# The row factors' turnings and the scaling with them two units later in a hybrid attention block

## What is computed

```python
p_cmp = masked_softmax(einsum(q, kc) * scale, cmp_mask)          # NSA: compressed keys
o_cmp = einsum(p_cmp, vc)
p = masked_softmax(einsum(q, k_sel) * scale, sel_mask)           # selected blocks ("slc")
o_slc = einsum(p, v_sel)
p = masked_softmax(einsum(q, kwin) * scale, win_mask)            # window of 512 ("win")
o_win = einsum(p, vwin)
y_a = g0 * o_cmp + g1 * o_slc + g2 * o_win                       # g: sigmoid gates per head
y_b = einsum(masked_softmax(einsum(q_b, k_top) * scale), v_top)  # DSA: indexer's top keys ("dsa")
merged = gate_a * (y_a @ w_branch_nsa) + gate_b * (y_b @ w_branch_dsa)
h = h + merged @ w_out
h = h + (silu(hn @ w_gate) * (hn @ w_up)) @ w_down
```

## Time and profile before

| | us |
|---|---|
| median of three runs | 1616.84 |
| lowest, highest | 1614.45, 1617.58 |
| profiled execution | 1614.37 |
| its span, first to last instruction | 1612.6 |

### The profile page before, as it was taken

One profiled execution on the slowest core, in us unless ns is written; L12 is line 12 of the kernel. 1 busy time (PEld: TensorE's weight loads), 2 busy tenths in 40 slices (PEclk: granted clock), 3 DMA queues, 4 the chain that ended last, 5 costly groups with the idle time before them and its releaser, 6 DMA issues.

```text
span 1612.6 us, 24584 instructions
## 1 busy us (share of the span) xinstructions
PE 1568.7 (97%) x9008; PEld 1326.2 (82%) x9008; DVE 1154.0 (72%) x2021; ACT 649.4 (40%) x1269; POOL 637.4 (40%) x442
## 2 busy tenths in 40 slices
PE   6999999999999999999999999999999999999997
PEld 5898888888799888999788887888888888887885
DVE  6745889999556678777674276677777766778978
ACT  5544322121566677766321244222222222343445
POOL 4234654221340244433221217444454444445454
PEclk9999999999999999999999999999999999999999
DMA  7033546331515010010345332333333334575533
GB/s 229 16 93 74 123 117 164 105 93 58 146 59 131 28 54 15 14 41 28 97 152 163 111 119 66 98 99 98 98 99 98 111 108 160 186 255 153 158 105 124
DMA packets 173303, 171.10 MB, mean 106 GB/s; under 512 B 25856, under 2 KB 126208, under 8 KB 173184
## 3 DMA queue, kind: packets, MB, share of 16 engines
q1 hardware_dynamic: 172896, 169.01, 34.8%
q10 hardware_dynamic: 288, 0.52, 0.1%
HBM read 122.04 MB, written 47.45 MB: 105 GB/s over the span
## 4 chain that ended last, share of the span: by engine, by line
PE 85%; DMA 6%; DVE 4%; issue 2%; POOL 2%; SPq 1%; ACT 1%; DVEq 0%; POOLq 0%; ACTq 0%
PE psA L1662 13%; PE psA L1664 13%; PE psA L1663 13%; PE psT L1664 9%; PE psT L1662 9%; PE psT L1663 9%; PE psT L1669 7%; PE psT L1883 5%; DMA wd<-in_w_down_dram 4%; PE psA L1772 3%; PE psA L1773 3%; PE psT L1898 1%; DMA w_raw<-in_w_in_dram 1%; DMA q<-scratch_q_dsa 1%; PE psT L1772 1%
## 5 line engine op out<-in xcount | busy, mean ns | idle before, releaser
L447 POOL TENSOR_TENSOR w_lo<-w_raw,w_hi 128x1024 fp32r<-128x1024 f32 (+2 forms) x52 | 119.9, 2307 | 255.4 <-ACT w_hi L442 255.1
L1258 POOL TENSOR_TENSOR w_lo<-w_sum,w_hi 128x1024 fp32r<-128x1024 f32 x44 | 115.4, 2628 | 119.4 <-ACT w_hi L1544 119.4
L1481 ACT ACTIVATE s<-s,nmax 128x640 f32<-128x640 f32 (+7 forms) x192 | 144.0, 752 | 28.6 <-DVE nmax L2360 27.2
L1282 POOL TENSOR_TENSOR w_lo<-act_raw,w_hi 128x512 fp32r<-128x512 f32 x77 | 107.3, 1394 | 106.9 <-ACT w_hi L1572 106.9
L1669 PE MATMUL psT<-ident,s 128*128 128x128 f32 x816 | 120.6, 278 | 0.8 <-ACT s L1481 0.8
L2450 DVE COPY pT<-psT 128x512 f32<-128x512 f32 (+1 forms) x116 | 69.6, 600 | 54.5 <-PE psT L1669 54.3
L2581 DVE TENSOR_TENSOR w_lo<-wd,w_hi 128x512 fp32r<-128x512 f32 x77 | 91.5, 1192 | 23.8 <-ACT w_hi L1579 23.4
L1669 PEld LDWEIGHTS psT<-ident,s 128*128 128x128 f32 x816 | 94.7, 142 | 16.7 <-issue 7.3
L442 ACT CAST w_hi<-w_raw 128x1024 fp32r<-128x1024 f32 (+2 forms) x52 | 52.6, 1015 | 138.4 <-PE psA L1664 81.4
L1572 ACT CAST w_hi<-act_raw 128x512 fp32r<-128x512 f32 x77 | 47.9, 622 | 125.3 <-PE psT L1664 64.7
L2250 DVE TENSOR_SCALAR_CACHE_REDUCE equal<-score,bit_try 128x512 f32<-128x512 f32 (+2 forms) x93 | 93.8, 1008 | 0.0
(11 more groups left out here) (380 smaller groups left out, 4668.8 us busy)
## 6 DMA issues: line engine op xcount, KB each, us to landing
act_raw<-scratch_act SPq DMA_DIRECT2D x77, 256.0 KB, 3.1
w_raw<-in_w_in_dram SPq DMA_DIRECT2D x24, 512.0 KB, 4.0
scratch_act<-act SPq DMA_DIRECT2D x33, 256.0 KB, 2.1
scratch_act<-act_sum SPq DMA_DIRECT2D x33, 256.0 KB, 2.1
wd<-in_w_down_dram SPq DMA_DIRECT2D x33, 256.0 KB, 3.1
scratch_gates<-gate_out SPq DMA_DIRECT2D x32, 256.0 KB, 3.0
gates<-scratch_gates SPq DMA_DIRECT2D x30, 256.0 KB, 4.2
a<-in_w_gate_dram SPq DMA_DIRECT2D x22, 256.0 KB, 3.2
```

What stands on the lines that cost most here:

```text
L447: nc.gpsimd.tensor_tensor(lo, raw, hi.bitcast(F32), ALU.subtract).then_inc(self.lo_done, 1)
L1258: nc.gpsimd.tensor_tensor(lo2[n % RING][:], block_of(n)[:], hi2[n % RING][:].bitcast(F32), ALU.subtract)\
L1282: nc.gpsimd.tensor_tensor(lo2[slot][:, 0:512], act_raw[n % 6][:], hi2[slot][:, 0:512].bitcast(F32), ALU.subtract)\
L1481: a_.activation(s_sb[v % SR][:, 0:n], s_sb[v % SR][:, 0:n], ACT.Exp, scale=-1.0, bias=nmax[:, BR[a], i, h:h + 1], accum_out=psum_p[:, BR[a ...
```

## The change

Four lines. A new lag `RT_LAG` = 8 takes the place of `O_LAG` = 6 for the turning of the row factors, in PE's program and in the list of bank groups. `F_LAG` goes from 7 to 9 and `Y_LAG` from 8 to 10, so that the scaling on DVE, the addition on POOL, and the rounding and remainder of the first half's tiles stand two steps later. The loop has two steps more. `O_LAG`, the copy of the sums, and the making of `r_wide` (lag 3) stay; the dsa chunks stay at step 198, the nsa chunks move from 199 to 201. SP's order is the same.

```diff
-    O_LAG, F_LAG, Y_LAG = T_LAG + 1 + V_LAG + 1, T_LAG + 1 + V_LAG + 2, 8
+    O_LAG, RT_LAG, F_LAG, Y_LAG = T_LAG + 1 + V_LAG + 1, T_LAG + 1 + V_LAG + 3, T_LAG + 1 + V_LAG + 4, 10
@@ the list of bank groups
-        if tile_of(u, O_LAG):
-            groups6.append(("r", *tile_of(u, O_LAG)))
+        if tile_of(u, RT_LAG):
+            groups6.append(("r", *tile_of(u, RT_LAG)))
@@ PE's program
-            if tile_of(u, O_LAG):
-                a, i = tile_of(u, O_LAG)
+            if tile_of(u, RT_LAG):
+                a, i = tile_of(u, RT_LAG)
                 pe.wait_ge(wide_done, t6[a, i] + 1)
```

## The result

| | before | after |
|---|---|---|
| median, us | 1616.48 (11 runs) | 1619.64 (11 runs) |
| lowest, highest | 1612.70, 1618.12 | 1617.24, 1623.45 |
| profiled execution | 1614.37 | 1620.57 |
| its span | 1612.6 | 1618.6 |

Ratio of the times, after by before: 1.0025, with a 95% interval of 1.0015 to 1.0035. The medians differ by 3.2 us, which is 0.20%, the means by 4.1 us, 0.25%. The forecast was 1.9 us slower, 1618.8 us; the measured median lies 0.8 us above it and inside the range of 1615.0 to 1622.8. By its own border of 0.2% the forecast said "same" first and "slower" second; 0.25% is just beyond that border, and the interval holds both sides of it.

What follows compares the result with a forecast made beforehand. TensorE, busy 97%, was taken to bound the kernel. Terms -2.9 - 1.7 + 0.4 + 5.2 + 0.9 make +1.9 us, 1616.3 against 1614.4, or 1618.8 us against the median of 1616.84; range 1615.0 to 1622.8.

Steps and rivals of the forecast that it cites:

- The last turning: End of attention: last row-factor turning falls behind a merging step, delaying the gates' loads and step 4; +5.2 us, 5.2 to 5.6.
- The clock at the end: Merging steps 3 and 4: PE's waits bring half-clock stretches, one perhaps uncovered; +0.9 us, between 0 and 1.7.
- The middle: Row-factor turnings before the end: PE's waits ahead of them shrink; -2.9 us, between 0 and -4.8.
- 558 and 576: First two window tiles' turnings: waits for POOL's wide row factors shrink, 0.7 of 1.74 and 1.0 of 1.24 us.
- 638.64: A turning that waited for DVE to empty a PSUM bank: PE goes on to scores, saving 1.0 of 1.40 us.
- The scalings at the new place: DVE's scaling now ahead of the compressed scores' bias, mostly covered; +0.4 us, between 0 and 1.4.
- The clock in the middle: Half-clock stretches at 560.8 and 577.8 us: one of the two goes; -1.7 us, between 0 and -3.4.
- The remainders: First half's rounding on ACT and remainders on POOL two units later: read much later, so nothing either way.
- the rivals the first: Middle gives little back, as scaling delays the chain to DVE's copy and half-clock stretches stay; 1622.6 us, chance 0.22.
- the second rival: Both waits at the end bring the half clock and both middle stretches stay; 1621.2 us, chance 0.13.
- the end would be covered: Gates' transfer quicker when issued later, or reload free otherwise, so the end costs 2 us or less; 1612.9 us, chance 0.08.
- the sign of the middle: Expected trace evidence: the stretch from 430 to 775 us becomes 3 to 5 us shorter.

Runs made afterwards that it cites:

- the last tile alone: Kernel before, with only the last selected tile's turning, scaling and chunks two units later: 1621.02 against 1617.08 us, ratio 1.0033.
- the block first: Changed kernel with the fourth weight block's rounding and remainder moved ahead of the nsa chunks: 1616.75 us, ratio 1.0007 to the kernel before.
- other copies: Changed kernel with copies of turned probabilities swapped, DVE taking even and ACT odd ones: 1622.78 us, ratio 1.0038 to the kernel before.
- the remainders: Kernel before, with only the first half's roundings and remainders two steps later: 1616.35 against 1617.08 us, ratio 1.0000.
- the block first alone: Kernel before, with only the fourth weight block's rounding and remainder moved ahead of the chunks, to step 198: 1616.73 against 1616.03 us, ratio 0.9998.
- all but the last tile: Changed kernel with the last tile's turning, scaling, addition and nsa chunks back at their old place: 1615.67 us, ratio 0.9997 to the kernel before.
- Without dsa: Kernel before, with only window and selected tiles 0 to 3 two units later: 1612.67 against 1615.60 us, ratio 0.9976.
- the first half alone: Kernel before, with only the dsa tiles and window and selected tiles 0 to 3 two units later: 1613.08 against 1617.08 us, ratio 0.9980.
- both: Kernel before, with dsa and first-half tiles two units later and the fourth weight block ahead of the chunks: 1612.22 against 1616.03 us, ratio 0.9980.

## Why the forecast was near, and where it failed

**The last turning, +5.2: right.** From step 0 to step 3 after loses 5.0 us. The chain is the one named, link by link: POOL's addition at 1.29 us and not 1.67 beside DVE (0.4 back, as forecast), gates' loads issued at 794.17 where 794.6 less the middle's gain of 0.24 was forecast, used 6.78 us later where before had 6.79. Step 3 waited 2.93 us in the shadow of step 4, against 3.3. The kernel with the last tile alone shows the term by itself at 4.1; its gates took 5.9 us from issue to use (794.80 to 800.69) and not 6.8. The kernel with the block first shows the link: with the gates' loads earlier 3.3 us go. The 4.1 and the 5.0 agree once the gates' time, 0.9 us shorter in that run, is taken into account.

**The clock at the end, +0.9: nothing.** A stretch behind the first wait, 2.93 us, came and lay under the second, as forecast. Windows of PE in after:

```profile
795.20:796.90 1.70, 1.70 (x6) 0.50 0.91 253
803.70:805.40 1.70, 1.70 (x9) 1.00 0.65 206
```

Since step 3 ran 3.4 us at half, it was 1.7 us longer, and the wait ahead of step 4 1.90 us and not over 3. Behind it the clock stayed at 1.00; the kernel with other copies had a stretch there, and in the kernel with the block first the one stretch lay uncovered. The rule of the Trainium skill that the forecast weighed (TensorE: Matmul & The Clock Gate, "HAM oscillation"), that PE kept waiting between bursts starts the next one at the lower clock, is borne out at 793.88 and not at 803.12.

**The middle, -2.9: the size of one place was right, of another not.** Between units 64 and 104, among kernels with one stretch at half there, those in the old order (the last tile, the remainders and the block first alone) are 1.1 to 1.2 us quicker than before and those with the move (all but the last tile, and the block first) 2.8. That is 1.6 us for the move, against 1.7 forecast for 558 and 576. The wait of 0.44 us, from which 0.2 was forecast, lies at the first dsa turning, at 430.98, outside of that stretch, and nothing is gained there that the traces show (see "Without dsa"). But the forecast had the first wait gone, and it is 0.77. Timelines of POOL and PE in after:

```profile
559.41 1.04 POOL L1207 TENSOR_TENSOR c_s<-c_s,c_st 128x512 f32<-128x512 f32 x1 [10.15 <-DVE c_st L2303]
560.41 1.04 POOL L1232 TENSOR_TENSOR row_factors_wide<-psum_r,nsa_gate 128x512 f32<-128x512 f32 x1
```

```profile
561.51 0.66 PE L1669 MATMUL psT<-ident,row_factors_wide 128*128 128x128 f32 x4 [0.77 <-POOL row_factors_wide L1232]
...
564.78 0.66 PE L1669 MATMUL psT<-ident,c_s 128*128 128x128 f32 x4 [0.74 <-POOL c_s L1213]
```

POOL's product ends at 561.45 and PE is there at 560.74. Two units of 128 keys took only 0.97 us off the wait (1.74 - 0.77); "two more units of PE work" should have been counted, not called enough. A new wait of 0.74 for `c_s`, also POOL's, follows. It stands in all five profiles that have no stretch at half there (after, the first half alone, other copies, both, without dsa; 0.40 to 0.74 us) and in none of the seven others: at half the clock PE comes too late to meet it. At 638.64 the forecast was 1.0 of 1.40. PE had scores to go on with, but then stood 0.50 and 0.36 us:

```profile
637.13 0.63 PE L1669 MATMUL psT<-ident,s 128*128 128x128 f32 x4 [0.50 <-DVE ya L2391]
...
639.22 0.63 PE L1669 MATMUL psT<-ident,row_factors_wide 128*128 128x128 f32 x4 [0.36 <-DVE pT L2450]
```

From unit 104 to unit 144 the gain is 0.2 us. A wait for a bank in rotation isn't taken away by going later in the order: the next thing that PE turns needs the next bank, and DVE is as far behind with it.

**The scalings at the new place, +0.4 (0 to 1.4): this step failed.** The forecast looked for a cost of the new place on DVE alone, in the scaling, and said that in the larger tiles "PE is behind it anyway"; to the turnings themselves it gave no cost in these tiles. What happens there is that the turning of row factors, which in before came right behind a turning whose bank had been left by then, now asks for a bank that is being copied: waits at 655.56 and 688.90, and smaller ones at the four others of these tiles. Counted from the start of PE's preceding instruction, less the 0.11 us that this takes in before, they make 2.1 us at the six turnings from 655 to 744 us. The differences agree: after goes from -2.18 to -0.24 between unit 144 and step 0, the kernel with the first half alone stays at -2.18. That is +1.9, outside the bounds. Swapping the copying engine doesn't cure it, and one unit less moves it to another turning and makes it smaller. The releaser in the rows is the copy and never the scaling, and at all six the scaling stands behind that copy. So it is the new place of the turnings that costs, not DVE's 0.69 us of scaling. No run moved the turning without the scaling.

**The clock in the middle, -1.7: right in the traces, partly luck.** After has neither stretch of the earlier trace rows. But the old order of that stretch had only one of them in all its three other profiles, and three of the eight with the move had one. From two to one it is worth 1.1 to 1.2 us (before against the last tile, the remainders and the block first alone), from one to none 0.6 (2.8 against 3.4 between units 64 and 104; 1.0 with the kernel without dsa, which has 3.8), not 1.7 each, since the wait for `c_s` takes its place.

**The remainders, 0: right**, ratio 1.0000.

Put together: 5.0 at the end, 1.9 in the second half, -1.6 and -0.2 in the middle, make +5.1, less 1.7 for the clock +3.4; the medians say +3.2, the forecast said +1.9. The errors were +1.5 for the turnings of the second half, +0.8 at 638.64, +0.1 at 558 and 576, +0.2 for the dsa wait, -0.9 for the clock at the end and -0.2 for the last turning, which is the 1.5 us between 1.9 and 3.4. That the forecast lay as near as it did is luck in part: the 0.9 expected of the clock didn't come, and made up for some of the 2.3 us of waits for banks that weren't foreseen. Of the rivals the first comes nearest in kind ("the middle gives little back"), but by another mechanism, the banks and not the chain through ACT, and its 1622.6 us is 3.0 us off. Of the second rival neither half came: one stretch at the end and not two, and none in the middle. That the end would be covered was wrong: the chain had no slack. Two numbers in the rivals' sums have no working: the first gives the middle 1.5 us without saying from what, and the third counts 4.6 where it speaks of 4.8. Neither changes which rival is nearest.

What was named as the sign of the middle, the stretch from 430 to 775 us 3 to 5 us shorter, didn't come: it is 2.1 us from unit 0 to step 0.

What pays of the change is win and slc of tiles 0 to 3: 0.9976 of before alone, and 0.9980 with dsa, with or without the block first, which the times can't tell apart.

## What to carry to other kernels

A lag that applies to every tile also applies to the last one, where nothing is left to hide it: here one turning of 24 cost 4 to 5 us in the traces because a chain of five engines hung on it, while the 23 others together cost nothing measurable. Split such a change by place before judging it; the tiles with small work gained 0.2% and those with large work gave it back. And a consumer moved later in a rotation of banks takes the place of another, so ask which bank it will find and when the copy before it ends, not only when its own input is ready.

## What the runs showed of the hardware

Stretches of TensorE at 1.2 GHz of 3.4 or 6.8 us come and go between executions of the same instructions. At 139 us there was one in after and in six of ten experiments, between 972 and 982 us one in after and in four experiments, and neither place has anything of the change. The one at 139 us is worth 1.1 to 2.2 us between two traces, as much as most parts looked for here; it takes the times, or several traces, to tell it from an effect. That its price can be 0.6 us for 3.4 us at half the rate was new too: a wait further on then isn't met.

DVE's product `merged` of two SBUF tiles took 0.69 us alone and 1.73 beside POOL's remainder of a weight block, which had begun 1.16 us before it (792.00 and 790.84 in the timelines of after, above). In 16 of the 32 such rows of before and after POOL's begins 0.13 to 0.19 us ahead, and the same product takes 2.76 to 2.83 us. In all 17 it ends 0.55 us after POOL's does; in the other 15, with nothing of POOL beside, it takes 0.69. The Trainium skill (SBUF — State Buffer, "SBUF: two separate sides") says that a DVE instruction with two SBUF inputs and a GpSimd instruction take one port pair in turns, the later one blocked until the other is through; these rows agree. The same was seen in the forecast's term of 0.4 us, from the other side: POOL's addition took 1.67 us beside DVE's remainders and 1.29 without them.
